# An fp32 chain of two transformer blocks, mLSTM and attention on one core: gate panels among the last mLSTM units, and four pieces of work in another order

## The reference, cut to what matters

```python
def first_block(...):                       # two layers l
    mod_lat = (silu(c) @ w_ada[l] + b_ada[l])           # six vectors of 1024: shift, scale, gate, twice
    h = modulate(rms_norm(x, g_attn[l]), sh1, sc1)
    gl, mq, mk, mv, nq, nk, nv = mixer_proj(h, ...)     # h @ w_in, then w_uq, w_ukv
    x = x + gt1 * gated_merge(gl, y_mla, y_na, w_mla_o[l], w_na_o[l], w_out[l])
    x = x + gt2 * squared_relu_mlp(modulate(rms_norm(x, g_mlp[l]), sh2, sc2), w_ff1[l], w_ff2[l])

def mlstm_mixer(...):                       # 4 heads, keys of 256, values of 512, both directions
    q, k, v, o, z, g = split(h @ w_in)
    h_sum = forward scan + backward scan                # here as masked scores times values
    hn = _head_rms(h_sum, head_g)
    return (sigmoid(o) * hn * silu(z)) @ w_out

def attn_mixer(...):                        # 16 query heads, 4 key heads, window and context, a sink
    q, k, v, z = split(h @ w_in); q, k = rope(rms_norm_2(q)), rope(rms_norm_2(k))
    return (softmax(...) @ v * silu(z)) @ w_out
```

## Time and profile before

| | us |
|---|---|
| median of 3 runs | 2168.86 |
| lowest and highest | 2168.02, 2169.65 |
| the profiled execution, its own time | 2168.83 |
| its span, first to last instruction | 2167.0 |
| TensorE busy in it | 2063.6 (95%) |

### The profile page before, as it was taken

The page is one execution under the profiler, slowest core; times in us unless marked ns, Lnnn a source line. Parts: engine busy times, 40 slices in busy tenths (PEclk is TensorE's granted clock), DMA queues, the critical chain, the costliest instruction groups (busy, mean ns, idle before and its releaser), DMA issues.

```text
span 2167.0 us, 32373 instructions
## 1 busy us (share of the span) xinstructions
PE 2063.6 (95%) x13298; PEld 1715.7 (79%) x13298; DVE 1138.3 (53%) x2228; ACT 903.5 (42%) x1639; POOL 83.9 (4%) x93
## 2 busy tenths in 40 slices
PE   4998999999999999999999899999999799999998
PEld 2898767687777777788779899987887477887877
DVE  4546672246433343465665776632566344445866
ACT  3435672234322231255564555433433232234565
POOL 1000000002000000110000100010000000001000
PEclk6998999999999999999999999999999999999999
DMA  7222004632444444344115454444211044222311
GB/s 282 95 79 77 35 35 166 223 136 78 162 187 157 182 168 165 148 164 180 54 55 217 153 194 177 176 161 165 103 45 59 25 170 158 95 97 78 137 40 40
DMA packets 47107, 277.20 MB, mean 128 GB/s; under 512 B 4464, under 2 KB 12784, under 8 KB 16752
## 3 DMA queue, kind: packets, MB, share of 16 engines
q1 hardware_dynamic: 42080, 266.94, 32.9%
q10 hardware_dynamic: 4736, 7.34, 1.0%
q0 software_dynamic: 144, 0.85, 0.1%
HBM read 273.01 MB, written 2.10 MB: 127 GB/s over the span
## 4 chain that ended last, share of the span: by engine, by line
PE 84%; DVE 8%; ACT 4%; DMA 2%; issue 1%; POOL 0%; SPq 0%; ACTq 0%; DVEq 0%
PE ps L552 18%; PE ps L553 17%; PE ps L554 17%; PE ps L589 4%; PE ps L591 4%; PE ps L590 4%; PE ps L669 3%; PE ps L619 3%; PE ps L701 2%; DVE t L1643 2%; PE ps L688 2%; PE ps L979 2%; DVE t L1661 2%; DVE t L1652 2%; DMA t<-in_panels 1%
## 5 line engine op out<-in xcount | busy, mean ns | idle before, releaser
L552 PE MATMUL ps<-t 128*128 128x512 f32 (+1 forms) x2232 | 780.0, 349 | 15.6 <-DVE t L1661 9.0
L553 PE MATMUL ps<-t 128*128 128x512 f32 (+1 forms) x2232 | 770.8, 345 | 0.0
L554 PE MATMUL ps<-t 128*128 128x512 f32 (+1 forms) x2232 | 770.3, 345 | 0.0
L1661 DVE TENSOR_TENSOR t<-t 128x1024 fp32r<-128x1024 f32 (+2 forms) x362 | 405.1, 1161 | 455.3 <-ACT t L1103 454.6
L1103 ACT ACTIVATE t<-t 128x1024 fp32r<-128x1024 f32 (+2 forms) x378 | 359.5, 1000 | 379.6 <-DMA t<-in_panels 299.9
L552 PEld LDWEIGHTS ps<-t 128*128 128x128 f32 x2232 | 422.8, 189 | 93.4 <-issue 15.6
L554 PEld LDWEIGHTS ps<-t 128*128 128x128 f32 x2232 | 422.7, 189 | 52.8
L553 PEld LDWEIGHTS ps<-t 128*128 128x128 f32 x2232 | 422.9, 189 | 50.2
L1643 DVE TENSOR_TENSOR t<-t 128x512 f32<-128x512 f32 (+9 forms) x637 | 249.3, 411 | 192.5 <-ACT t L1192 49.7
L589 PE MATMUL ps<-t 128*128 128x256 f32 (+1 forms) x812 | 241.4, 297 | 0.3 <-DVE t L1661 0.3
L590 PE MATMUL ps<-t 128*128 128x256 f32 (+1 forms) x812 | 234.8, 289 | 0.0
(11 more groups left out here) (150 smaller groups left out, 1771.5 us busy)
## 6 DMA issues: line engine op xcount, KB each, us to landing
t<-in_panels SPq DMA_DIRECT2D x236, 1024.0 KB, 4.8
t<-in_panels SPq DMA_DIRECT2D x19, 512.0 KB, 4.3
t<-in_panels SPq DMA_DIRECT2D x6, 768.0 KB, 4.5
t<-in_window ACTq DMA_DIRECT2D x4, 768.0 KB, 4.3
t<-in_ctxT SPq DMA_DIRECT2D x1, 1024.0 KB, 12.6
t<-in_xT SPq DMA_DIRECT2D x1, 1024.0 KB, 14.8
t<-in_ctxT ACTq DMA_DIRECT2D x1, 1024.0 KB, 5.7
t<-in_xT ACTq DMA_DIRECT2D x1, 1024.0 KB, 7.3
```

Of the source, the lines that this page charges most:

```text
L552: e.matmul(o, hi[:, k, w], xh[:, c0:c1], start=k == 0, stop=False)
L553: e.matmul(o, hi[:, k, w], xl[:, c0:c1], start=False, stop=False)
L554: t = e.matmul(o, lo[:, k, w], xh[:, c0:c1], start=False, stop=k == p.nk - 1)
L1661: e.tensor_tensor(p.half(wlo[p.buf], a), p.half(raw[p.slot], a), p.half(whi[p.buf], a).bitcast(F32), ALU.subtract).then_inc(*up(ve, ("lo", ...
```

## The change

1. **Condition vectors at the start.** TensorE does ada 0 to 6 ahead of the norm sums and ada 7 behind them. ScalarE copies the first row of PSUM between its squares.
2. **The first panel's split.** cq leaves POOL_PANELS. ScalarE makes its high part behind the second shift, VectorE its low part behind the first `left`.
3. **The first layer's condition panels.** AFTER puts them behind "gm", "gn", "mo" of all four heads, none behind "no". There are twelve as before.
4. **mLSTM.** LSTM_PIECES becomes a list by step: the pieces of step 12 go from 3 to 2, of 13 from 2 to 1, and steps 14 and 15 get one each; in the last head the tokens 0 to 255 of both value panels come first (LSTM_VALUES). `output_gate` does mo (0), mo (1) and mz (0), a group each, in steps 16, 17 and 18 into held banks; the condition panel behind mo stands in step 17. ScalarE and VectorE split mv 7 at step 10, mo 0 at 14, mz 0 at 15. The transposed result is read by ScalarE (`out(key, hnT...)`, ahead of the next unit's square), without the gain, which VectorE applies later in the product with the sigmoid. `select(0)` stands earlier.
5. **Attention.** VectorE's `gate(0)` stands ahead of the rotation of the second half.

The diff, cut; `pieces = list(LSTM_VALUES)` and `left = LSTM_PIECES[i]` stand on all three engines. The tables and TensorE:

```diff
-AFTER = ([(kind, 0, h) for h in range(3) for kind in ("gm", "gn", "mo", "no")]
+AFTER = ([(kind, 0, h) for h in range(4) for kind in ("gm", "gn", "mo")]
...
-LSTM_PIECES = {3: 3, 0: 3, 1: 2, 2: 0}
+LSTM_VALUES = ([(h, a, tile) for h in range(3) for a in range(2) for tile in range(4)]
+               + [(3, 0, 0), (3, 0, 1), (3, 1, 0), (3, 1, 1), (3, 0, 2), (3, 0, 3), (3, 1, 2), (3, 1, 3)])
+LSTM_PIECES = [3, 2, 0, 3, 3, 2, 0, 3, 3, 2, 0, 3, 2, 1, 1, 1, 0, 0, 0]
...
-POOL_PANELS = [("cq", 0, 0), ("uq", 0, 0), ("ff1", 0, 0), ("ckv", 1, 0), ("uq", 1, 0), ("ff1", 1, 0), ("mq", 0), ("atkv", 0)]
+POOL_PANELS = [("uq", 0, 0), ("ff1", 0, 0), ("ckv", 1, 0), ("uq", 1, 0), ("ff1", 1, 0), ("mq", 0), ("atkv", 0)]
...
+                def output_gate(kind, j):
+                    p = at[kind, 0]
+                    if j == 0:
+                        weights(p)
+                    weight_left((kind, j), j, p, xa, 0, hold=True)
+                    if j == 1:
+                        used(p)
+                ahead = {16: ("mo", 0), 17: ("mo", 1), 18: ("mz", 0)}
...
-                    left = LSTM_PIECES[i % 4] if i < 15 else 0
+                    left = LSTM_PIECES[i]
                     if left:
                         project()
                         left -= 1
+                    if i in ahead:
+                        output_gate(*ahead[i])
...
-                        if tile == 0:
-                            e.wait_ge(*done(("v out", h)))
+                        if tile % 2 == 0:
+                            e.wait_ge(*done(("v out", h, tile + 1)))
...
                 mark(pe, "lstm end")
+                for x in ahead.values():
+                    banks.give(x)
...
-            for i in range(4):
+            for i in range(AT_START - 1):
                 ada(i)
             for x in "cl":
                 rms("n1.0", x)
-            for i in range(4, AT_START):
-                ada(i)
+            ada(AT_START - 1)
```

ScalarE, at the start and in the mLSTM:

```diff
                 if not l:
-                    hi_to(at["cq", 0, 0].i)
                     for x in "cl":
                         for k in range(8):
                             shifted(s, k, x, "b", 0, 0)
+                            if x == "c" and k == 1:
+                                hi_to(at["cq", 0, 0].i)
...
+                    if i == 10:
+                        hi_to(at["mv", 7].i)
+                    if i == 14:
+                        hi_to(at["mo", 0].i)
+                    if i == 15:
+                        hi_to(at["mz", 0].i)
+                    if i >= 3:
+                        h, tile = LSTM_UNITS[i - 3]
+                        key = ("hT", i - 3)
+                        out(key, hnT[:, 4 * h:4 * h + 4, tile * 128:tile * 128 + 128], banks(key).rearrange("p (c t) -> p c t", t=128))
```

VectorE, in the mLSTM and in the attention layer:

```diff
-                    if i >= 3:
-                        h, tile = LSTM_UNITS[i - 3]
-                        key = ("hT", i - 3)
-                        e.wait_ge(*done(("full", key)))
-                        tt(hnT[:, 4 * h:4 * h + 4, tile * 128:tile * 128 + 128], banks(key).rearrange("p (c t) -> p c t", t=128),
-                           S("mlhg")[:, 4 * h:4 * h + 4].unsqueeze(2).to_broadcast([128, 4, 128]), ALU.mult, ("read", key))
+                    if i == 10:
+                        lo_to(at["mv", 7].i)
+                    if i == 14:
+                        lo_to(at["mo", 0].i)
+                    if i == 15:
+                        lo_to(at["mz", 0].i)
...
-                            tt(hnT[:, c, :], hnT[:, c, :], s1[j][:, :], ALU.mult)
+                            stt(hnT[:, c, :], hnT[:, c, :], S("mlhg")[:, c:c + 1], s1[j][:, :], ALU.mult, ALU.mult)
...
                     begin(at["atz", 0] if half else at["atq", 2])
+                    if half:
+                        gate(0)
                     for tile in range(2):
```

More of the change, by code:

```diff
@@ L2047, in lstm_layer, with select @@
                 e.wait_ge(s_zone, 16)
+                def select(h):
+                    for dr in range(2):
+                        if h:
+                            e.wait_ge(*done(("full", ("bro", h - 1, dr))))
+                        e.tensor_copy(sel[dr][:, :], ident[0:8, dr * 4 + h:dr * 4 + h + 1].to_broadcast([8, 128])).then_inc(
+                            *up(ve, ("sel", h, dr)))
                 zf, zb = Z("zf"), Z("zb")
@@ L2211, in rotated, with gate @@
                     rope(v[:, :, 0:32], v[:, :, 32:64], tab, tm, *names)
+                def gate(a):
+                    for c in range(2 * a, 2 * a + 2):
+                        e.wait_ge(*done(("asig", c)))
+                        tt(sz[:, c, :], banks(("atz", c))[:, 0:256], sz[:, c, :], ALU.mult, ("read", ("atz", c)))
                 begin(at["atkv", 0])
@@ L2246, in attention_layer @@
                             begin(at["atq", 3])
-                def gate(a):
-                    for c in range(2 * a, 2 * a + 2):
-                        e.wait_ge(*done(("asig", c)))
-                        tt(sz[:, c, :], banks(("atz", c))[:, 0:256], sz[:, c, :], ALU.mult, ("read", ("atz", c)))
-                for a in range(3):
-                    if a:
-                        begin(at["atz", a])
+                for a in range(1, 3):
+                    begin(at["atz", a])
                     gate(a)
```

55 lines of the change are left out of this document (24 added, 31 removed).

## The result

| | before | changed |
|---|---|---|
| median, us | 2168.70 | 2144.45 |
| lowest and highest of four runs | 2168.02, 2169.65 | 2142.51, 2146.62 |
| profiled execution, its own time | 2168.83 | 2142.51 |
| its span | 2167.0 | 2140.7 |
| TensorE busy in it | 2063.6 | 2053.9 |

The ratio is 0.9883 with a 95% interval of 0.9871 to 0.9895. Forecast were 2145.0 and a range of 2139.5 to 2152.0. Where such a difference comes from is left open: none of the longer executions has a trace.

The account below looks back on a forecast made before the run. TensorE, busy 2063.6 of 2167.0 us, bounds the kernel, so only its idle and low-clock time can be won. Gains of 5.0 + 3.7 + 10.1 + 5.0 = 23.8 from 2168.83 give 2145.0, range 2139.5 to 2152.

Parts of the forecast that it names:

- The chain: At the start, condition vectors, norm sums, ada 7, its row's add and the first product hang together; 5.0 us won.
- the 1.7: At the start, behind the first product: 2.9 us regained, less 1.2 for VectorE's own second half of the split.
- the 2.9: At the start, time two VectorE instructions lose beside GpSimd's split: 3.83 us where elsewhere they take 0.45 each.
- the 4.9: At the start, us from VectorE's add of ada 7's row to the first product, the same before and after.
- the 0.9 of the lock: At the start, VectorE's new split could be locked out by GpSimd's rest of k = 1, lowering the sum by 0.9 us.
- Wait (a): mLSTM, ahead of unit 12's transposes: TensorE still waits 2.6 us for the scaled result.
- Wait (b): mLSTM, mz 0's second group: TensorE waits 2.9 us for mo 0's bank, behind ScalarE's copy, table load and sigmoid.
- All covered: Rival, chance 0.15: both remaining mLSTM waits, at unit 12 and at mz 0, are absorbed; 2139.5 us.
- Half of the tail: Rival, chance 0.15: ScalarE sets the rhythm of mLSTM steps 14 to 18, units 13 and 14 wait too; 2152 us.
- Not as said: Rival, chance 0.05: held banks block, mLSTM gate groups run behind the waits, the tail gives 1 us; 2154 us.
- The slower rival: Rival, chance 0.02: two mLSTM waits bring the clock down and it stays down between them; 2173 us.
- The forecast's own ends: Whole kernel: the four terms' ends taken half way, since they rarely miss together; 2140.5 and 2150 us.

Follow-up runs that it names:

- the filled start: The changed kernel with 36 transposes of the identity in TensorE's idle stretch of 5.56 us ahead of the first product: 2149.31 us, ratio 0.9903.
- the order alone: The changed kernel with cq's split as before (high part ahead of the first shift, low part on GpSimd), keeping the new condition vector order: 2146.72 us, ratio 0.9893.
- the mLSTM alone: The kernel before with only the mLSTM part of the change: 2165.2 us, ratio 0.9970.
- the kernel without the three waits: The changed kernel with mo 0 and mz 0 splits and mo 0's sigmoids moved, and the bank turn moved by four: 2139.77 us, ratio 0.9852.
- the early sigmoid: The changed kernel with mo 0's two sigmoids, and the table load, taken in steps 16 and 17 behind the squares: 2143.43 us, ratio 0.9873.
- attention alone: The kernel before with only gate(0) moved ahead of the rotation: 2166.1 us, ratio 0.9973.
- start alone: The kernel before with only the new condition vector order and first panel's split: 2167.1 us, ratio 0.9976.

## Why the prediction was right

**Start (5.0 forecast, 6.2 found).** The chain was the right one, two sizes in it were not, and they have opposite signs. Ada 7 was put at 33.3, "3.0 later" than the sums (that is the distance from the first sum, not from the second as the text has it). It ran at 31.84, 0.6 behind the second sum, and was no longer on the path, the reciprocals were, and the row was added at 34.77 instead of 35.9; from that add to the first product it was 4.64 where 4.9 was taken. The clock was up sooner (1.00 from 25.0 on; ada 5 and 6 took 1.07 instead of 1.94 us each), but that is not what won: TensorE then waited 0.68 and 1.40 for those two panels, and the sums began at 29.95 where 30.3 was forecast. Behind the first product 1.1 came of the 1.7. The low clock is not the reason, for with the clock at 1.00 the filled start needs the same 16.50 us; the 2.9 was counted whole behind the first product, although the first stretched instruction stands ahead of it, inside the 4.9. The sum lies inside the ends of 3.0 and 6.5. VectorE's new split took 2.36 us for two pieces, as the 1.16 of the profile's page, so the 0.9 of the lock did not come. This does not speak against the rule of the SBUF — State Buffer page of the Trainium skill (Who interferes with whom), since GpSimd's piece had ended before the split began. The rule shows elsewhere in the same trace, in the other direction, where GpSimd's root of unit 13 takes 1.40 us beside VectorE's split of mz 0:

```profile
1685.03 2.35 DVE L1689 TENSOR_TENSOR t<-t 128x1024 fp32r<-128x1024 f32 x2
```

```profile
1685.26 1.40 POOL L2328 TENSOR_TENSOR t<-t 128x1 f32<-128x1 f32 x1
```

The same instruction takes 0.57 in the next steps.

**First layer's condition panels (3.7 forecast, 4.0 found).** Right, as worked out. Nothing was late behind them. The 0.3 more is the third wait, 0.29 at 433.65, which neither the rows nor the sum had. Against other executions with the old list the term is larger, up to 8.6, since the waits that it removes differ (2.57 to 4.16 at gm of head 2, 0.29 to 2.31 at the third place), and behind three of them the clock fell.

**mLSTM (10.1 forecast, 11.0 found).** Wait (a) was forecast at 2.6 and is 2.55, though TensorE and the square both came 0.3 to 0.4 us earlier behind unit 14's scores than was worked out (12.1 and 12.0 instead of 12.4), and the square's way to TensorE was 2.73 instead of 2.55. Wait (b) was forecast at 2.9 and is 2.60: no table load was followed by a drain, the sigmoid begins 0.01 us behind the load's end. So the trace speaks against the 1.38 us that the page ScalarE: Activation LUTs (What ACT_TABLE_LOAD costs) of the Trainium skill adds, and against the sum of 8.7 by it. From unit 14's scores to the first product of the attention layer TensorE's idle time fell from 12.95 to 5.94, 7.0 us. The other 4.0 is shorter matmul time, where the sum had 3.4 for the clock; the two low stretches that went (1694.2 to 1697.6 and 1701.1 to 1704.5) can give no more than 3.4, and the 0.6 has no cause here. That both waits would leave the clock alone is what the forecast assumed. Five traces have both waits: in three (the changed kernel twice, the order alone) the clock stayed, in the mLSTM alone it fell behind (a), in the filled start behind both. That is worth up to 3.0 us and is the part of the forecast that was luck. It can make at most half of the 4 us between the shortest and the longest run of the result, whose mean clock is the same 0.989.

**Attention (5.0 forecast, 5.0 found).** No wait over 0.2 is left at atz 1 and 2, where 0.3 and 0.2 were taken; the two gate panels take 11.5 us at 1.00. Followed matmul by matmul in both traces, the first matmul of atz 1's group 0 stands 4.5 us nearer to the layer's first product, the clock gives 1.5 (1.7 was taken, but the first matmuls of atz 1 in the kernel before still ran at 1.00), 0.2 goes at atz 2, and the bank shift costs 0.8: 5.0. The part alone, which has no shift, won 5.8. One more low stretch of the kernel before, from 2004.8 to 2008.3, is gone in both and gave nothing: TensorE lost 1.5 us in it, then waited 0.23 for the layer's second panel where now it waits 1.26, and by 2011.3 the two traces are level. So the terms were the right ones, and two errors of 0.2 cancel: the wait at atz 1 gave 4.5 where 4.63 - 0.3 was taken, the clock 1.5 where 1.7 was.

**Rivals.** "All covered" (2139.5) is near what the kernel without the three waits measured, 2139.8, but that kernel is without the wait at the first scores too. For (a) and (b) alone the traces give 4.9 (2.05 + 2.84) where the rival had 5.5, and its mechanism needed the edits to both. "Half of the tail" did not happen: ScalarE sat idle for 2.7 to 6.6 us at a time in steps 16 to 18. "Not as said" fell with the mLSTM alone. The slower rival would have needed the low clock to stay; where it fell behind these waits it was back 3.4 us later. The forecast's own ends are not half way as said: half of the four terms' ends gives 2142.2 and 2149.2, not 2140.5 and 2150. The stated range does not hang on it.

## What to carry to other kernels

Where an in-order engine serves a chain and prepares the next panel too, put the chain's link first: the split ahead of the square cost 2.05 us, and moving one split alone only handed 0.76 of it to the next unit. Do the first instruction that needs another table while the engine idles, and count banks when groups are moved: a shift by two cost 0.87 us two stages later and one line gave it back. Low clock cost only where TensorE set the pace: dummy transposes won 1.6 us among the second layer's transposes, and nothing in two stages in which VectorE set it.

## What the runs showed of the hardware

- The same wait may or may not bring the clock down: behind the 2.55 to 2.57 us of unit 12 it stayed at 1.00 in four profiled executions (the changed kernel twice, the early sigmoid, the order alone) and was at 0.50 in two (the mLSTM alone, the filled start). Nor does the length order them: at gm it stayed behind 3.25 and 3.00 (before, attention alone) and was at 0.50 behind 2.57 and 2.31 (mLSTM alone) and 4.16 (start alone).
- 36 transposes in an idle stretch of 5.5 us held the clock at 1.00 through it and through the panel behind it (one execution); without them it was at 0.50 from 35.2 to 45.5.
- A GpSimd instruction on 128x1 elements took 1.40 us instead of 0.57 beside a VectorE split of 128x1024.
- The first transfer's landing differs by up to 2.4 us between executions (the first condition panel at 7.70 to 10.09), and what comes behind shifts with it; a difference of 1 or 2 us between kernels is better read from distances within a trace than from medians of four runs.
